# A tuned two-block network on one core: norm factors by tokens, the end on turned tokens, one weight unit split ahead of ada work

## The chip, the cores and the metric

The kernel runs on 1 core of one Trainium2 chip. The metric is the device time of one launch in microseconds (us). Each version is run three times or more, and the median counts. In the traces PE is the matmul engine (TensorE), DVE is VectorE, ACT is ScalarE, POOL is GpSimd and SP is SyncE. PEld is the loading of stationary operands into PE.

## What is computed

256 tokens of 1024 features go through two blocks, everything in float32. The first puts 16 meta tokens ahead, mixes by window means and a gated linear attention, and has a two-level mixture of experts. The second has two layers (l0, l1) over the 256 tokens `h` and 256 context tokens `hc`. The kernel spends most of its time there, and most of the change lies there.

```python
def _rms_norm(x, g):
    return x * lax.rsqrt(jnp.mean(x * x, axis=-1, keepdims=True) + EPS) * g
def _modulate(u, shift, scale):
    return u * (1.0 + scale) + shift
def _swiglu(u, w_gate, w_up, w_down):
    return (jax.nn.silu(u @ w_gate) * (u @ w_up)) @ w_down

h = rmsnorm(first_block(x, ...), final_norm_w)
for l in range(2):
    mod_x = silu(c) @ w_ada[l] + b_ada[l]     # nine vectors: shift, scale, gate of three sublayers
    h = h + 0.5 * g1 * _swiglu(_modulate(_rms_norm(h, norm_ffn1[l]), sh1, sc1), ffn1 weights)
    q, k, v = _modulate(_rms_norm(h, norm_mix[l]), shm, scm) @ w_in[l]
    h = h + gm * (attention(q, k, v, context) @ w_out[l])
    h = h + 0.5 * g2 * _swiglu(_modulate(_rms_norm(h, norm_ffn2[l]), sh2, sc2), ffn2 weights)
    # hc goes the same way with its own modulation; in the last layer only its keys and values count
return _rms_norm(h, norm_final)
```

## The kernel before

Activations lie turned. A tile has 128 features on the partitions and the tokens on the columns, 256 or 512 of them, and eight such rows make up the 1024 features. A product in float32 is made from two halves of each operand, high and low. `products` issues three matmuls for it: high by high (L1763), high weights by low rows (L1764) and low weights by high rows (L1765).

**Weights.** They stream through the kernel in units of up to 128x2048 elements (1 MB) in two slots. SP loads `raw`. ACT casts it to `w_hi` (`split_hi`, L589). DVE subtracts and gets `w_lo` (`split_lo`, L990). PE begins a unit when `lo_done` has reached it. A slot is loaded again when the high and the low part of the unit before it are done, and cast again when PE has finished with it. The order of each engine is written out by hand, stage by stage, and a counting semaphore joins each producer with its consumer.

**Ada work.** The modulation vectors `mod` are products of two single vectors (`c` and `c_ctx`) with the 75.5 MB of `w_ada`. ACT's queue loads a quarter chunk (`ada_load`, L607, when DVE is done with the one before it in that slot), DVE multiplies and adds (`ada_quarter`, L1008 and L1011), PE sums over partitions (`ada_sums`, L1930) and DVE adds the bias (L1020). These pieces are spread over the other stages. In `linear`, which does the query units and the out units, DVE takes the two accumulated tiles of a unit (L1559), does the ada quarters of that unit, and then makes `w_lo` for the unit two ahead.

**Norms.** The feature squares come from ACT (L615), and POOL sums six or seven of the eight rows in `sq_sum` (L1699). PE multiplies `ones_d` (a 128x128 matrix of 1/1024, in `base`) by the sum and by the last squares. That gives the mean on all partitions, 128x256 of it in a PSUM bank (`mean_of_sums` L1786, `mean_square` L1780, `half_mean_squares` L1821). ACT takes the root (L671, L638 or L653), and DVE the reciprocal, 128x256 in `rstd` (L1083, L1046 or L1026). Then DVE makes eight scaled rows `tmp_a` (`scaled_row`, L1069), ACT casts them and adds the shift (`high_rows`, L715, `u_hi`), and DVE makes their low part `u_lo` (`low_row`, L1076). The norms of the second block work in two halves, 256 tokens and 256 context tokens. The products that close the stage before (`close_down`, `close_linear`) and the first products of the next (`open_halves`) run around them. The norms have names: `ffn1` ahead of the router of the first block, `l0a`, `l0b`, `l0c` ahead of ffn1, attention and ffn2 of layer 0, `l1a`, `l1b`, `l1c` in layer 1, and `end2` at the end.

**The end.** After the last products of ffn2 of layer 1, DVE adds the last row to `h` (L1195) and ACT squares it. The norm `end2` follows on all of the eight rows. PE turns the result back to tokens on partitions (16 transposes, L1756), DVE copies it out of PSUM in four pieces (L1666), and SP stores it with one DMA (L568).

## Time and profile before

| | us |
|---|---|
| median of 3 runs | 2278.59 (2275.73 to 2281.95) |
| the profiled execution | 2279.42 |
| its span in the trace | 2277.7 |
| PE busy | 2192.4 |
| DVE busy | 1388.2 |
| ACT busy | 766.8 |
| POOL busy | 519.5 |

All times inside the program are from the profiled execution, in us from the start of its span. Its own time stands 1.7 above its span, and 0.8 above the median. The mean granted clock of PE over the span is 0.98 of full speed. A PE that waits shows as a gap between its rows, and the view of waits puts each gap down to the instruction that ended it.

### The profile page before, as it was taken

The page shows a single profiled execution, that of the slowest core. Times are in us where ns is not written, and L with a number is a line of the kernel's source. Part 1 is how long each engine was busy: PE and PEld are TensorE (multiplying, and loading weights), DVE is VectorE, ACT ScalarE, POOL GpSimd, SP SyncE. Part 2 cuts the span into 40 slices and gives each one's busy share as a digit, 9 for nine tenths or more (in the row PEclk, how much of TensorE's full clock was granted, in tenths as well). Part 3 has the DMA queues.
Part 4 walks back from the last instruction along what each step waited for, and adds up shares of the span by engine and source line. Part 5 has one row for each costly group of instructions (what it writes and reads, how often), then busy time and mean ns, then how long its engine had stood idle before and what let it go on. Part 6 is the DMA issues. An engine that isn't in the chain of part 4 may idle for free.

```text
span 2277.7 us, 31630 instructions
## 1 busy us (share of the span) xinstructions
PE 2192.4 (96%) x13181; PEld 1903.3 (84%) x13181; DVE 1388.2 (61%) x1780; ACT 766.8 (34%) x1073; POOL 519.5 (23%) x243
## 2 busy tenths in 40 slices
PE   7988999999999999999999999999999998999997
PEld 7868999988888888857888888888888887678997
DVE  5567877577776237695677773256654236765444
ACT  4334344432222222273422222142222223454443
POOL 0013633112221110153122221112222111143431
PEclk9889999999999999999999999999999999999999
DMA  5236886656664335401366652346663335205654
GB/s 160 93 94 166 219 220 193 182 160 182 172 174 135 89 103 174 111 20 39 101 191 174 177 167 82 105 112 185 185 185 113 96 90 168 74 12 153 181 165 121
DMA packets 473989, 314.67 MB, mean 138 GB/s; under 512 B 27488, under 2 KB 435943, under 8 KB 473847
## 3 DMA queue, kind: packets, MB, share of 16 engines
q1 hardware_dynamic: 434288, 237.02, 37.2%
q10 hardware_dynamic: 39558, 75.64, 10.7%
q8 instruction: 104, 1.70, 0.3%
q14 instruction: 39, 0.31, 0.0%
HBM read 311.56 MB, written 1.05 MB: 137 GB/s over the span
## 4 chain that ended last, share of the span: by engine, by line
PE 84%; DVE 9%; ACT 3%; DMA 1%; issue 1%; SPq 1%; POOL 0%; ACTq 0%; DVEq 0%; POOLq 0%
PE ps L1763 25%; PE ps L1765 25%; PE ps L1764 25%; DVE w_lo L990 3%; PE ps L1930 2%; ACT w_hi L589 2%; PE ps L1756 2%; PE ps L2340 1%; DVE st L1605 1%; DVE u_lo L1076 1%; PE ps L2302 1%; DVE tmp_a L1069 1%; DMA raw<-in_w_in 1%; SPq L562 1%; DMA raw<-in_w_ffn_down 1%
## 5 line engine op out<-in xcount | busy, mean ns | idle before, releaser
L1763 PE MATMUL ps<-u_hi,w_hi 128*128 128x256 f32 (+2 forms) x2624 | 890.0, 339 | 29.4 <-DVE w_lo L990 15.9
L1765 PE MATMUL ps<-u_hi,w_lo 128*128 128x256 f32 (+2 forms) x2624 | 878.1, 335 | 0.0
L1764 PE MATMUL ps<-u_lo,w_hi 128*128 128x256 f32 (+2 forms) x2624 | 878.0, 335 | 0.0
L990 DVE TENSOR_TENSOR w_lo<-raw,w_hi 128x2048 fp32r<-128x2048 f32 (+1 forms) x238 | 504.5, 2120 | 339.8 <-ACT w_hi L589 339.6
L589 ACT CAST w_hi<-raw 128x2048 fp32r<-128x2048 f32 (+1 forms) x238 | 418.0, 1757 | 468.9 <-PE ps L1765 420.5
L1763 PEld LDWEIGHTS ps<-u_hi,w_hi 128*128 128x128 f32 x2624 | 502.9, 192 | 84.1 <-DVE w_lo L990 21.8
L1765 PEld LDWEIGHTS ps<-u_hi,w_lo 128*128 128x128 f32 x2624 | 502.8, 192 | 48.8
L1764 PEld LDWEIGHTS ps<-u_lo,w_hi 128*128 128x128 f32 x2624 | 503.3, 192 | 46.9
L1684 POOL TENSOR_TENSOR hf_lo<-tmp_b,hf_hi 128x512 fp32r<-128x512 f32 (+1 forms) x88 | 240.4, 2732 | 715.5 <-ACT hf_hi L729 715.5
L1011 DVE SCALAR_TENSOR_TENSOR ada_acc<-ada_w,sc_c,ada_acc 128x512 f32<-128x512 f32 x448 | 347.4, 832 | 5.5
L726 ACT ACTIVATE tmp_a<-ps 128x512 f32<-128x512 f32 (+1 forms) x120 | 60.2, 501 | 704.9 <-PE ps L1765 540.5
L1763 PE MATMUL ps<-hf_hi,w_hi 128*128 128x512 f32 (+1 forms) x770 | 271.0, 352 | 1.3 <-DVE w_lo L990 1.1
L1764 PE MATMUL ps<-hf_lo,w_hi 128*128 128x512 f32 (+1 forms) x770 | 269.4, 350 | 0.0
L1765 PE MATMUL ps<-hf_hi,w_lo 128*128 128x512 f32 (+1 forms) x770 | 269.4, 350 | 0.0
L1137 DVE TENSOR_TENSOR tmp_b<-tmp_a,ps 128x512 f32<-128x512 f32 (+1 forms) x120 | 68.2, 568 | 183.6 <-ACT tmp_a L726 182.5
L1763 PEld LDWEIGHTS ps<-hf_hi,w_hi 128*128 128x128 f32 x770 | 144.9, 188 | 23.1 <-DVE w_lo L990 1.3
L1764 PEld LDWEIGHTS ps<-hf_lo,w_hi 128*128 128x128 f32 x770 | 144.9, 188 | 21.0
L1765 PEld LDWEIGHTS ps<-hf_hi,w_lo 128*128 128x128 f32 x770 | 144.9, 188 | 20.9
L1699 POOL TENSOR_TENSOR sq_sum<-sq_sum,tmp_b 128x512 f32<-128x512 f32 (+1 forms) x37 | 75.4, 2038 | 299.9 <-ACT tmp_b L615 252.5
L1744 POOL TENSOR_SCALAR s<-s,st 128x512 f32<-128x512 f32 (+1 forms) x48 | 78.9, 1646 | 141.8 <-DVE st L1620 141.8
L1684 POOL TENSOR_TENSOR hm_lo<-tmp_b,hm_hi 128x256 fp32r<-128x256 f32 x32 | 77.7, 2428 | 133.8 <-ACT hm_hi L729 133.8
L1195 DVE SCALAR_TENSOR_TENSOR h<-ps,gate,h 128x256 f32<-128x256 f32 x50 | 22.3, 480 | 104.3 <-PE ps L1765 104.3
(299 smaller groups left out, 1886.1 us busy)
## 6 DMA issues: line engine op xcount, KB each, us to landing
ada_w<-in_w_ada ACTq DMA_DIRECT2D x144, 512.0 KB, 3.9
raw<-in_w_ffn_gate SPq DMA_DIRECT2D x88, 512.0 KB, 4.0
raw<-in_w_ffn_up SPq DMA_DIRECT2D x88, 512.0 KB, 5.3
raw<-in_w_in SPq DMA_DIRECT2D x52, 512.0 KB, 4.9
raw<-in_w_ffn_down SPq DMA_DIRECT2D x64, 384.0 KB, 3.5
raw<-in_w_ffn_down SPq DMA_DIRECT2D x64, 320.0 KB, 4.2
raw<-in_w_expert_gate SPq DMA_DIRECT2D x32, 512.0 KB, 4.3
raw<-in_w_expert_up SPq DMA_DIRECT2D x32, 512.0 KB, 5.6
```

The source lines that it names most:

```text
L589: nc.scalar.copy(w_hi[:, slot, 0:elems], raw[:, slot, 0:elems]).then_inc(hi_done.sem, 1)
L726: nc.scalar.activation(tmp_a[:, n % 2, 0:T], ps[:, 2 * (g % 2), 0:T], ACT.Silu).then_inc(sig["silu"].sem, 1)
L990: tt(w_lo[:, slot, 0:elems], raw[:, slot, 0:elems], w_hi[:, slot, 0:elems].bitcast(F32), ALU.subtract).then_inc(lo_done.sem, 1)
L1011: ins = stt(out=ada_acc[:, v, :], in0=ada_w[:, slot, kk, :], scalar=sc_c[:, k, v:v + 1], in1=ada_acc[:, v, :], op0=ALU.mult, op1=ALU.add)
L1137: tt(tmp_b[:, n % 2, 0:T], tmp_a[:, n % 2, 0:T], ps[:, 2 * (g % 2) + 1, 0:T], ALU.mult).then_inc(acc_free.sem, 1)
L1684: tt(lo[:, n, 0:T], tmp_b[:, n % 2, 0:T], hi[:, n, 0:T].bitcast(F32), ALU.subtract).then_inc(sig["lo"].sem, 1)
L1699: tt(sq_sum[:, 0:T], sq_sum[:, 0:T], tmp_b[:, k % 2, 0:T], ALU.add).then_inc(n["summed"].sem, 1)
L1744: ins = nc.gpsimd.tensor_scalar(s[:, x, 1, c0:c1], s[:, x, 1, c0:c1], st[:, i % 4, 0, nq + q:nq + q + 1], None, ALU.mult)
L1756: return nc.tensor.transpose(dst, src, ident[0:n, 0:n])
L1763: mm(acc, w1, m_hi, start=(first and i == 0), stop=False)
L1764: mm(acc, w1, m_lo, start=False, stop=False)
L1765: ins = mm(acc, w2, m_hi, start=False, stop=(last and i == n - 1))
```

## The change

**Norms by tokens.** In `ffn1`, `l0b`, `l0c`, `l1a`, `l1b`, `l1c` and the latent half of `l0a` the mean is taken with the operands exchanged. The sums and squares are stationary, and one column of `ones_d` moves (`token_means`). The mean stands by tokens, 128 on the partitions and two columns for 256 tokens. ACT's root and DVE's reciprocal work on these two columns (`tok_inv`). PE then spreads the factor (`spread_factor`): a column of `tok_inv`, broadcast to 128x128, is stationary and the identity moves. The factor stands in a PSUM bank for 256 tokens on all partitions, where the scaled rows read it. The separate mean of the sums for both halves (`sums_of_halves`) goes, and the reciprocal of the second half moves from behind `w_lo` to ahead of it.

**The end.** ACT scales each row of `h` by the final weight as soon as it has been squared (`out_row`, into `h1`, which is free by then). PE turns it between the last products (`turn_out`). After the last row, mean, root and reciprocal are taken by tokens, on two columns. ACT and DVE each scale one half of the turned result by the token's factor on the way out of PSUM, and SP stores it with two DMAs.

**`linear`.** For the first unit of each of its stages, DVE makes `w_lo` ahead of the ada quarters.

```diff
+        BY_TOKENS = ("ffn1", "l0b", "l0c", "l1a", "l1b", "l1c")
...
-            sp.wait_ge(rows_out.sem, rows_out.at(12 + 4))
-            sp.dma_start(out[0].rearrange("(t p) d -> p t d", p=P), o_rows[:, :, :]).then_inc(st_out, 16)
-            sp.wait_ge(st_out, 16)
+            for t in range(2):
+                sp.wait_ge(ev["out_left"], t + 1)
+                sp.wait_ge(ev["out_right"], t + 1)
+                sp.dma_start(out[0, P * t:P * t + P, :], o_rows[:, t, :]).then_inc(st_out, 16)
+            sp.wait_ge(st_out, 32)
...
-                nc.scalar.activation(rstd[:, 0:T], ps[:, 5, 0:T], ACT.Sqrt, bias=eps).then_inc(n["root"].sem, 1)
+                if nm in BY_TOKENS:
+                    nc.scalar.activation(tok_inv[:, 0, :], ps[:, 5, 0:2], ACT.Sqrt, bias=eps).then_inc(n["root"].sem, 1)
+                else:
+                    nc.scalar.activation(rstd[:, 0:T], ps[:, 5, 0:T], ACT.Sqrt, bias=eps).then_inc(n["root"].sem, 1)
...
             def half_root(nm, q):
 
-                n, (c0, c1, v), F = norm_of[nm], HALVES[nm][q], WHOLE[nm]
-                act.wait_ge(n["ms"].sem, n["ms"].at((q + 1) * (KD - F)))
-                nc.scalar.activation(rstd[:, c0:c1], ps[:, 5 + q, c0:c1], ACT.Sqrt, bias=eps).then_inc(n["root"].sem, 1)
+                n = norm_of[nm]
+                act.wait_ge(n["ms"].sem, n["ms"].at(q + 1))
+                nc.scalar.activation(tok_inv[:, q, :], ps[:, 5 + q, 0:2], ACT.Sqrt, bias=eps).then_inc(n["root"].sem, 1)
 
...
+            def out_row(n):
+
+                k = n // 2 - 1
+                if n % 2 == 0 and k >= 0:
+                    w = VEC["final2"][0] + k
+                    nc.scalar.activation(h1[:, k, 0:SEQ], h2[:, k, 0:SEQ], ACT.Identity,
+                                         scale=vec[:, w:w + 1]).then_inc(norm_of["end2"]["w"].sem, 1)
...
+            n = norm_of["end2"]
+            act.wait_ge(acc_free.sem, acc_free.at(end_of(layers[1]["f2b"])))
+            square("end2", KD - 1, 1, h2, SEQ)
+            out_row(2 * KD)
+            act.wait_ge(n["ms"].sem, n["ms"].at(1))
+            nc.scalar.activation(row_inv[:, :], ps[:, 4:6, 0:1].rearrange("p t o -> p (t o)"), ACT.Sqrt,
+                                 bias=eps).then_inc(n["root"].sem, 1)
+            act.wait_ge(turned.sem, turned.at(11))
+            act.wait_ge(n["rstd"].sem, n["rstd"].at(1))
+            for t in range(2):
+                nc.scalar.activation(o_rows[:, t, 0:512], ps[:, OUT_BANKS[t][0], :], ACT.Identity,
+                                     scale=row_inv[:, t:t + 1]).then_inc(ev["out_left"], 1)
...
             def half_rstd(nm, q):
 
-                n, (c0, c1, v) = norm_of[nm], HALVES[nm][q]
+                n = norm_of[nm]
                 dve.wait_ge(n["root"].sem, n["root"].at(q + 1))
-                nc.vector.reciprocal(rstd[:, c0:c1], rstd[:, c0:c1]).then_inc(n["rstd"].sem, 1)
-                dve.wait_ge(n["rstd"].sem, n["rstd"].at(q + 1))
+                nc.vector.reciprocal(tok_inv[:, q, :], tok_inv[:, q, :]).then_inc(n["rstd"].sem, 1)
 
             def rows_from(nm, t0, q, k0, k1, ahead=2):
 
+                dve.wait_ge(norm_of[nm]["spread"].sem, norm_of[nm]["spread"].at(q + 1))
...
-                stt(out=scaled(q, k, c1 - c0), in0=(h2 if h is None else h)[:, k, first + c0:first + c1], scalar=s, in1=rstd[:, c0:c1],
+                stt(out=scaled(q, k, c1 - c0), in0=(h2 if h is None else h)[:, k, first + c0:first + c1], scalar=s,
+                    in1=rstd[:, c0:c1] if nm == "l0a" and q == 0 else ps[:, 5 + q, 0:SEQ],
...
                         add_half(1).then_inc(acc_free.sem, 1)
+                    if k == 5 and not whole:
+                        half_rstd(nm, 1)
                 if second and not whole:
                     split_lo(convert[-1], convert[-1] % 2, elems_of[convert[-1]])
-                if not whole:
-                    half_rstd(nm, 1)
                 if second and not whole:
                     rows_from(nm, t0, 1, 0, KD)
...
                     take(i, ps[:, 2 * (g % 2):2 * (g % 2) + 2, :]).then_inc(acc_free.sem, 1)
+                    convert = u + 2 < N_UNITS and not (keep_last and i == stg["units"] - 1)
+                    if convert and i == 0:
+                        split_lo(u + 2, u % 2, elems_of[u + 2])
                     for c, quarter in work:
                         ada_quarter(c, quarter)
-                    if u + 2 < N_UNITS and not (keep_last and i == stg["units"] - 1):
+                    if convert and i:
                         split_lo(u + 2, u % 2, elems_of[u + 2])
                     if behind:
...
-                nc.vector.tensor_copy(o_rows[:, t // 2, 512 * (t % 2):512 * (t % 2) + 512], ps[:, 2 + t, :]).then_inc(rows_out.sem, 1)
+            n = norm_of["end2"]
+            dve.wait_ge(n["root"].sem, n["root"].at(1))
+            nc.vector.reciprocal(row_inv[:, :], row_inv[:, :]).then_inc(n["rstd"].sem, 1)
+            dve.wait_ge(n["rstd"].sem, n["rstd"].at(1))
+            dve.wait_ge(turned.sem, turned.at(11))
+            for t in range(2):
+                ts(o_rows[:, t, 512:D], ps[:, OUT_BANKS[t][1], :], row_inv[:, t:t + 1], None,
+                   ALU.mult).then_inc(ev["out_right"], 1)
...
+            def token_means(nm, bank, c0, last):
+
+                for t in range(2):
+                    a = c0 + P * t
+                    mm(ps[:, bank, t:t + 1], sq_sum[:, a:a + P], ones_d[:, 0:1], start=True, stop=False)
+                    for (need_sq, slot, c) in last:
+                        if t == 0:
+                            need_sq()
+                        ins = mm(ps[:, bank, t:t + 1], tmp_b[:, slot, c + P * t:c + P * t + P], ones_d[:, 0:1], start=False,
+                                 stop=slot == 1)
+                return ins
+
+            def spread_factor(nm, q, bank, slot):
+
+                n = norm_of[nm]
+                pe.wait_ge(n["rstd"].sem, n["rstd"].at(q + 1))
+                for t in range(2):
+                    ins = mm(ps[:, bank, P * t:P * t + P], tok_inv[:, slot, t:t + 1].to_broadcast([P, P]), ident[:, :],
+                             start=True, stop=True)
+                ins.then_inc(n["spread"].sem, 1)
...
             def half_mean_squares(nm, q):
 
                 n, (c0, c1, v), F = norm_of[nm], HALVES[nm][q], WHOLE[nm]
-                for k in range(F, KD):
+
+                def squared(k):
                     pe.wait_ge(n["sq"].sem, n["sq"].at(k + 1 + q * (KD - F)))
-                    mm(ps[:, 5 + q, c0:c1], ones_d, tmp_b[:, k % 2, c0:c1], start=False, stop=(k == KD - 1)).then_inc(n["ms"].sem, 1)
+                pe.wait_ge(n["summed"].sem, n["summed"].at(F))
+                token_means(nm, 5 + q, c0, [(lambda k=k: squared(k), k % 2, c0) for k in range(F, KD)]).then_inc(n["ms"].sem, 1)
...
-                        ins = products(acc, uA % 2, [P * k for k in range(cut, kt2)], rows[cut:kt2], c1 - c0, False, False)
+                        products(acc, uA % 2, [P * k for k in range(cut, 7)], rows[cut:7], c1 - c0, False, False)
+                        spread_factor(nm, 0, 5, 0)
+                        ins = products(acc, uA % 2, [P * k for k in range(7, kt2)], rows[7:kt2], c1 - c0, False, False)
...
+            def turn_out(n):
+
+                k = n // 2 - 2
+                if n % 2 or k < 0:
+                    return None
+                w = norm_of["end2"]["w"]
+                pe.wait_ge(w.sem, w.at(k + 1))
+                for t in range(2):
+                    ins = turn(ps[:, OUT_BANKS[t][k // 4], P * (k % 4):P * (k % 4) + P], h1[:, k, P * t:P * t + P], P)
+                return ins
...
-            norm("end2", SEQ, KD - 1)
-
-            src = h2
-            w = norm_of["end2"]["w"]
-            pe.wait_ge(w.sem, w.at(8))
-            for t in range(4):
-                for k in range(4):
-                    kk = 4 * (t % 2) + k
-                    c = P * (t // 2)
-                    ins = turn(ps[:, 2 + t, P * k:P * k + P], src[:, kk, c:c + P], P)
-                ins.then_inc(turned.sem, 1)
+            n, tail = norm_of["end2"], (KD - 1) % 2
+            pe.wait_ge(n["summed"].sem, n["summed"].at(WHOLE["end2"]))
+            for t in range(2):
+                mm(ps[:, 4 + t, 0:1], sq_sum[:, P * t:P * t + P], ones_d[:, 0:1], start=True, stop=False)
+            pe.wait_ge(n["sq"].sem, n["sq"].at(KD))
+            for t in range(2):
+                ins = mm(ps[:, 4 + t, 0:1], tmp_b[:, tail, P * t:P * t + P], ones_d[:, 0:1], start=False, stop=True)
+            ins.then_inc(n["ms"].sem, 1)
+            turn_out(2 * KD)
+            turn_out(2 * KD + 2).then_inc(turned.sem, 1)
```

DVE at the first query units of layer 0 (`proj_107` is where the two accumulated tiles of a unit go), before and with the change:

```order
L1559 TENSOR_SCALAR proj_107<-ps 128x1024 [waits unit_done,dve_chain]
L1008 TENSOR_SCALAR ada_acc<-ada_w,sc_c 128x512 [waits ada_sum,ada_full_0]
L1008 TENSOR_SCALAR ada_acc<-ada_w,sc_c 128x512
L1011 SCALAR_TENSOR_TENSOR ada_acc<-ada_w,sc_c,ada_acc 128x512 [waits ada_mac] x2
L1011 SCALAR_TENSOR_TENSOR ada_acc<-ada_w,sc_c,ada_acc 128x512 [waits ada_mac,ada_full_1]
L1011 SCALAR_TENSOR_TENSOR ada_acc<-ada_w,sc_c,ada_acc 128x512 [waits ada_mac] x3
L990 TENSOR_TENSOR w_lo<-raw,w_hi 128x2048 [waits hi_done]
L1559 TENSOR_SCALAR proj_107<-ps 128x1024 [waits unit_done]
```

```order
L1598 TENSOR_SCALAR proj_107<-ps 128x1024 [waits unit_done,dve_chain]
L1018 TENSOR_TENSOR w_lo<-raw,w_hi 128x2048 [waits hi_done]
L1036 TENSOR_SCALAR ada_acc<-ada_w,sc_c 128x512 [waits ada_sum,ada_full_0]
L1036 TENSOR_SCALAR ada_acc<-ada_w,sc_c 128x512
L1039 SCALAR_TENSOR_TENSOR ada_acc<-ada_w,sc_c,ada_acc 128x512 [waits ada_mac] x2
L1039 SCALAR_TENSOR_TENSOR ada_acc<-ada_w,sc_c,ada_acc 128x512 [waits ada_mac,ada_full_1]
L1039 SCALAR_TENSOR_TENSOR ada_acc<-ada_w,sc_c,ada_acc 128x512 [waits ada_mac] x3
L1598 TENSOR_SCALAR proj_107<-ps 128x1024 [waits unit_done]
```

The `w_lo` of the third query unit has moved ahead of two L1008 and six L1011 (now L1036 and L1039), and it now stands right behind the first `proj_107`.

DVE around the second half of the norm `l0b`, before and with the change. In the new rows `ps` is the bank that holds the spread factor:

```order
L1069 SCALAR_TENSOR_TENSOR tmp_a<-h,coef,rstd 128x256 [waits norm_lo]
L1076 SCALAR_TENSOR_TENSOR u_lo<-tmp_a,mod,u_hi 128x256 [waits norm_hi] x2
L990 TENSOR_TENSOR w_lo<-raw,w_hi 128x2048 [waits hi_done]
L1083 RECIPROCAL rstd<-rstd 128x256 [waits norm_root]
L1069 SCALAR_TENSOR_TENSOR tmp_a<-h,coef,rstd 128x256 [waits norm_lo,norm_rstd]
L1069 SCALAR_TENSOR_TENSOR tmp_a<-h,coef,rstd 128x256 [waits norm_lo]
L1076 SCALAR_TENSOR_TENSOR u_lo<-tmp_a,mod,u_hi 128x256 [waits norm_hi]
```

```order
L1103 SCALAR_TENSOR_TENSOR tmp_a<-h,coef,ps 128x256 [waits norm_lo]
L1118 RECIPROCAL tok_inv<-tok_inv 128x2 [waits norm_root]
L1111 SCALAR_TENSOR_TENSOR u_lo<-tmp_a,mod,u_hi 128x256 [waits norm_hi] x2
L1018 TENSOR_TENSOR w_lo<-raw,w_hi 128x2048 [waits hi_done]
L1103 SCALAR_TENSOR_TENSOR tmp_a<-h,coef,ps 128x256 [waits norm_lo,factor_spread]
L1103 SCALAR_TENSOR_TENSOR tmp_a<-h,coef,ps 128x256 [waits norm_lo]
L1111 SCALAR_TENSOR_TENSOR u_lo<-tmp_a,mod,u_hi 128x256 [waits norm_hi]
```

The reciprocal has gone from 256 columns to two and from behind `w_lo` to ahead of the last two `u_lo`. The first scaled row of the second half now waits for PE (`factor_spread`).

PE at the very end, before and with the change:

```order
L1765 MATMUL ps<-hf_hi,w_lo 128x256
L1786 MATMUL ps<-sq_sum,base 128x256 [waits norm_summed]
L1780 MATMUL ps<-tmp_b,base 128x256 [waits norm_sq]
L1756 MATMUL ps<-base,h 128x128 [waits norm_w]
L1756 MATMUL ps<-base,h 128x128 x15
```

```order
L1807 MATMUL ps<-hf_hi,w_lo 128x256
L2471 MATMUL ps<-base,sq_sum 128x1 [waits norm_summed]
L2471 MATMUL ps<-base,sq_sum 128x1
L2474 MATMUL ps<-base,tmp_b 128x1 [waits norm_sq]
L2474 MATMUL ps<-base,tmp_b 128x1
L1798 MATMUL ps<-base,h 128x128 [waits norm_w]
L1798 MATMUL ps<-base,h 128x128
L1798 MATMUL ps<-base,h 128x128 [waits norm_w]
L1798 MATMUL ps<-base,h 128x128
```

The two matmuls of 256 columns are four of one column, and of the sixteen transposes four are left here. The other twelve now stand between the products of the last units, in pairs.

## Rows read from the trace of the kernel before

**Rows 1.** The page's first part: busy time of each engine, share, instructions

```profile
PE 2192.4 (96%) x13181; PEld 1903.3 (84%) x13181; DVE 1388.2 (61%) x1780; ACT 766.8 (34%) x1073; POOL 519.5 (23%) x243
```

**Rows 2.** Waits of PE: what for; us in total, times, longest

```profile
PE ps L1763 <- DVE w_lo L990: 20.2, 13, 5.9
PE ps L1763 <- DVE u_lo L1076: 9.3, 8, 4.1
```

**Rows 3.** Timeline, the end: start, us, engine, line, instruction [idle before <-releaser]

```profile
2260.38 0.48 DVE L1195 SCALAR_TENSOR_TENSOR h<-ps,gate,h 128x256 f32<-128x256 f32 x1 [4.54 <-PE ps L1765]
...
2261.36 0.70 PE L1780 MATMUL ps<-tmp_b,base 128*128 128x256 f32 x2 [0.59 <-ACT tmp_b L615]
2262.10 0.47 ACT L653 ACTIVATE rstd<-ps,base 128x256 f32<-128x256 f32 x1 [0.79 <-PE ps L1780]
2262.61 1.75 DVE L1026 RECIPROCAL rstd<-rstd 128x256 f32<-128x256 f32 x1 [1.75 <-ACT rstd L653]
...
2268.82 3.68 PE L1756 MATMUL ps<-base,h 128*128 128x128 f32 x16 [6.75 <-ACT h L660]
...
2272.53 0.69 DVE L1666 COPY o_rows<-ps 128x512 f32<-128x512 f32 x1 [0.16 <-PE ps L1756]
2273.25 0.39 SPq L568 DMA_DIRECT2D out<-o_rows  x1
```

**Rows 4.** The chain in order of time, two pieces: start, us, what

```profile
892.37 1.68 PE ps L1930 x16
...
1020.71 1.02 PE ps L1756 x8
```

**Rows 5.** Groups by form, DVE: count | busy, mean ns | idle before

```profile
L1020 DVE TENSOR_TENSOR mod<-ps,b_ada 128x8 f32<-128x8 f32 x28 | 4.4, 156 | 11.0 <-PE ps L1930 11.0
...
L1195 DVE SCALAR_TENSOR_TENSOR h<-ps,gate,h 128x256 f32<-128x256 f32 x50 | 22.3, 480 | 104.3 <-PE ps L1765 104.3
...
L1069 DVE SCALAR_TENSOR_TENSOR tmp_a<-h,coef_fin,rstd 128x256 f32<-128x256 f32 x8 | 3.7, 478 | 0.0
```

**Rows 6.** Timeline, ACT, a root on one column

```profile
2199.16 0.20 ACT L733 ACTIVATE root_one<-base 128x1 f32<-128x1 f32 x1
```

**Rows 7.** Timeline, ACT, early in the last stage (ffn2 down, layer 1)

```profile
2225.56 1.37 ACT L589 CAST w_hi<-raw 128x1408 fp32r<-128x1408 f32 x1 [4.00 <-DMA raw<-in_w_ffn_down]
```

**Rows 8.** Timeline, DVE, first query units of layer 0

```profile
871.36 1.22 DVE L1559 TENSOR_SCALAR proj<-ps 128x1024 f32<-128x1024 f32 x1 [3.20 <-PE ps L1765]
...
873.29 4.06 DVE L1011 SCALAR_TENSOR_TENSOR ada_acc<-ada_w,sc_c,ada_acc 128x512 f32<-128x512 f32 x6
877.27 2.29 DVE L990 TENSOR_TENSOR w_lo<-raw,w_hi 128x2048 fp32r<-128x2048 f32 x1
```

**Rows 9.** Timeline, ACT and its queue, the same stretch

```profile
871.34 1.90 ACT L589 CAST w_hi<-raw 128x2048 fp32r<-128x2048 f32 x1 [3.78 <-PE ps L1765]
874.73 3.03 ACTq L607 DMA_DIRECT2D ada_w<-in_w_ada  x2
```

**Rows 10.** Windows: A:B us, busy PE, PEld, DVE, ACT, POOL, PEclk, DMA share, GB/s

```profile
877.00:879.60 2.60, 0.01 (x1) 0.00 (x0) 2.60 (x3) 1.74 (x1) 0.00 (x0) 1.00 0.69 179
879.60:882.00 2.40, 2.39 (x7) 1.85 (x8) 2.40 (x4) 0.15 (x1) 0.00 (x0) 0.60 0.83 238
```

**Rows 11.** Tile ada_w, 860 to 930 us: landing time of its DMAs

```profile
DMA to landing us min/median/max: 3.6/3.8/5.2
```

**Rows 12.** Timeline, DVE, the norm l1c

```profile
2062.63 1.75 DVE L1083 RECIPROCAL rstd<-rstd 128x256 f32<-128x256 f32 x1 [2.17 <-ACT rstd L671]
```

**Rows 13.** Timeline, ACT, behind the root of the norm ffn1

```profile
150.91 1.89 ACT L589 CAST w_hi<-raw 128x2048 fp32r<-128x2048 f32 x1
```

**Rows 14.** Timeline, PE, means of the sums in the norm l0c

```profile
1101.65 1.13 PE L1786 MATMUL ps<-sq_sum,base 128*128 128x256 f32 x4 [0.73 <-POOL sq_sum L1699]
```

**Rows 15.** Timeline, DVE, second half of the norm l0b

```profile
857.13 2.28 DVE L990 TENSOR_TENSOR w_lo<-raw,w_hi 128x2048 fp32r<-128x2048 f32 x1
```

**Rows 16.** Timeline, ACT, the norm l1b

```profile
1883.51 3.69 ACT L589 CAST w_hi<-raw 128x2048 fp32r<-128x2048 f32 x2
```

79 lines of the change are left out of this document (42 added, 37 removed).

## The prediction

> **What bounds the kernel now.** Read in this order: the busy shares, the list of who waited for whom on PE, then the timeline at each norm. PE is busy 96% of the span [rows 1]. A change that takes work off DVE or ACT therefore pays only where PE stands still. PE's own waits are short and of two kinds: for the low part of a weight unit (w_lo, DVE), 20.2 us in 13 waits, and for the low part of a normalized row (u_lo, DVE), 9.3 us in 8 [rows 2]. Beside these stands the end, where PE has no products left: from the last accumulate, 2260.38, to the end of the span, 2277.7, are 17.3 us in which one engine after the other works [rows 3]. The reciprocal over 128x256 is the longest piece, 1.75 us; the eight scaled rows follow, then 3.68 us of turning, the last copy, and the store, whose issue stands 4.45 us before the end.
>
> **The prices** [rows 4 to 6]. A float32 matmul with one moving column costs two records: 16 records of the ada sums take 1.68 us, 0.105 each, so 0.21 per matmul. A 128-column transpose takes 0.13 (8 in 1.02). A float32 matmul of 128 columns has two such records; I take 0.26, so a spread of two costs 0.52. A small DVE instruction takes 0.16 us (128x8), a small ACT one 0.20. So root and reciprocal on two columns take 0.36 instead of 0.47 + 1.75, and the spread adds 0.52 and a semaphore's way of about 0.1: the chain from mean to first row gets 1.2 us shorter. The reciprocal on two columns itself is in no row; its bounds are the 0.16 and the 1.75, and I take 0.16, since duration goes with columns in every other DVE row.
>
> **The end.** Before, as above, 17.3 us. After: the accumulate and the square stay (to 2261.3, where the mean began at 2261.36 [rows 3]), two one-column matmuls 0.45, root 0.25, reciprocal 0.2: the factor is there at 2262.25. The rows are already scaled by the weights and turned, the last pair while root and reciprocal run; the last row's ACT scaling (0.5) ends at 2261.8 and delays neither. Two DVE passes of 128x512 at 0.69 end at 2263.7, ACT's two beside them earlier. From the issue of the store to the end took 4.45 us for 1 MB; now half of it leaves 0.7 us earlier. Bounds 3.6 and 4.45, taken 4.0: end at 2267.7, **10.0 us saved**. Against it stand twelve transposes between the products of the last stage. Early in that stage the weights come late (ACT waits 4.0 us for a DMA [rows 7], and PE waits for w_lo just behind it), which covers the first four; eight at 0.13 are new work on a full PE: **+1.0**. The added ACT row (0.5 us, seven times before the last products) goes into waits of 2 to 4 us as in [rows 7] and costs nothing; without that cover it would push w_hi, and so PE, by up to 3.5. Net −9.0, bounds −7 and −10.5.
>
> **The third query unit of layer 0.** DVE takes the products of the first unit at 871.36, then does 4.9 us of ada work to 877.35, and only then w_lo for the third [rows 8], though ACT had w_hi ready at 873.25 [rows 9]. PE stands from 877.0 to 879.6 and then runs at a granted clock of 0.60 from 879.6 to 882 [rows 10], the lower of the two levels for part of it: the wait of 2.6 us costs a further 1.7 (the unit took 12.7 us where the next took 11.0). With w_lo first it is done at 875.6 and both go: −4.3. What is late next: ada work now ends near 880.4, so the second pair of ada loads, which ACT issued at 874.73 and again at 877.4 [rows 9], is issued some 3 us later, the second at 880.4. A load lands in 3.6 to 5.2 us [rows 11], here beside 1 MB of weights, so at 884 to 885.6; ACT's cast for the fourth unit stands behind that issue, and DVE's w_lo for it behind the ada work: 2.7 us more, then 2.3, so 889 to 890.7. PE comes free of the third unit at 888.1, does the ada sums until 889.9 and waits at most 0.8. Fourth unit 3.3 to 4.0 us earlier: I take −3.7; bounds −1 (if the clock falls again) and −4.3. The out stage of layer 0 is turned round in the same way; PE waits for nothing there, so it counts zero.
>
> **The norms inside the kernel.** Each saves only what its last-ending wait lets go:
> - Before ffn2 of layer 1 (l1c) PE has nothing else: its wait for u_lo is 4.1 of the 9.3 us, and the 1.75 of the reciprocal stands in it [rows 2, 12]. The chain shortens by 1.2; everything behind is tied to the DVE rows: −1.2.
> - Before the router (ffn1) the same chain, but ACT's cast of a weight unit follows the root, 150.91 to 152.8 [rows 13]. It now begins 0.25 earlier, and the first u_hi waits for it: −0.8 instead of −1.2. In l0a the same pattern gives −0.4.
> - Ahead of ffn2 in layer 0 (l0c) PE waited 0.73 for the sums and spent 1.13 on them, in front of half a unit's products [rows 14]. Sums move behind those products. Gone: 1.5 (with overlap) and 1.03 of means; come: six matmuls of 0.21 and one spread of 0.52: −0.8, and the rest of that closing is tied to it.
> - l0b and l1a: −0.2 each by the same count with four one-column matmuls. The second half's reciprocal leaves DVE, but it stood behind the w_lo PE waits for, which begins at 857.13 because of the rows ahead of it [rows 15]. The new small reciprocal falls into a gap there, the new spread into PE's wait of 1.2. So nine of the large reciprocals go and most were hidden anyway.
> - l1b: here the reciprocal stands ahead of w_lo, and 1.75 would go. But ACT's two casts start at 1883.51, the first ends 1885.4 [rows 16], and w_lo started at 1885.8: −0.4. ACT is late next.
> Together −3.2 − 0.8 = **−4.0**: 1.2 + 0.8 + 0.4 + 0.8 + 0.4 + 0.4.
>
> **A rule against it.** The scaled rows now read the factor from PSUM. In the rows a 128x256 scalar_tensor_tensor takes 480 ns with PSUM as source and 478 without [rows 5]: I charge nothing. The Trainium skill, page "VectorE: DVE Perf Modes", section "The TRN2 errata", gives VectorE a fixed term of 120 cycles for a PSUM source against 58 for SBUF, which at 0.96 GHz would be an estimated 65 ns more for each row, 3.6 us in seven places of eight rows. The rows of this trace disagree with it.
>
> **Sum.** −9.0 − 3.7 − 4.0 = −16.7. The profiled execution took 2279.42 (span 2277.7), 0.8 above the median of 2278.59; against the median, **2261.9 us**, −0.73%. About 0.3%, 6.8 us, is what a measurement of this kernel can tell from no change.
>
> **Rivals.**
> - A (12%): the query stage gives its gain back. For it: ada loads and 1 MB of weights share the DMA engines. Against: the landings of 3.6 to 5.2 us were measured beside such a load. One wait of 2.7 at the fourth unit, with a clock loss of 1.0 kept: 2265.6.
> - B (9%): PSUM as a source slows the rows. Rows of this very shape differ by up to 50 ns between groups; eight rows in seven chains that DVE bounds: +2.8, 2264.7. The page named above would put it at 2265.5.
> - C (8%): ACT's extra rows and the transposes hold up the last stage, whose weights already come late: seven times 0.5 in front of w_hi: +3.5, 2265.4.
> - D (7%): the clock. Every shift moves the stretches at the lower level; each one that falls onto products costs about 1.7 as in the query stage. Two more: 2265.3; two fewer: 2258.5.
> - E (4%), slower: PE now holds the round trip. Each of the ten spreads inside the program waits in PE's queue for ACT and DVE, with all products behind it. If the small reciprocal comes behind a w_lo of 2.29 us [rows 8], PE loses that each time: +22.9 − 16.7 = +6.2, 2284.8. It decides from an average loss of 1.7 us per spread. Against it: four to six products' time stands between mean and spread, 1.4 us or more, and the chain needs 0.5.
> - F (2%): the small reciprocal and root take as long as the large (a fixed cost). Then the end gives 8, the query stage 3.7, and the norms lose the spreads: 2268.
>
> **Numbers.** The forecast has 58%. A to D lie within 4 us of it. The range 2256.5 to 2269.0 takes in the bounds of the end (+2/−1.5), of the query stage (+2.7/−0.6), one or two shifts of the clock (1.7 each) and the median's own scatter (the three runs span 6 us); outside are E, F and the tails, 2 in 10. Faster by over 0.3%: forecast, A to D and F less a tail, 0.93; within 0.3%: 0.03; slower: 0.04.
>
> **What would show it.** After the last product about 7.5 us instead of 17.4; two stores; transposes in pairs between products. No PE wait for w_lo at the third query unit, a granted clock of 1.0 behind it, and the fourth unit starting within 1 us of the ada sums' end. Reciprocals of 0.16 us, spreads of 0.5. PE's wait for u_lo in l1c split in two, 2.8 in all; the waits of 1.0 and 1.2 in l0b and l1a still there; l1b's 3.0 down to about 2. It is wrong if PE stalls ahead of the spreads by more than 0.3 us each, if the rows take over 0.5 us, or if the last stage takes more than 1.5 us longer.

## The result, and the profile after

The changed kernel takes 2264.75 us (median of 5 runs, 2263.07 to 2266.74), the kernel before 2280.28 in the same measurement. The ratio is 0.9935, 95% interval 0.9922 to 0.9948. Run a second time unaltered, it took 2266.47 us, ratio 0.9947 (0.9935 to 0.9959). The forecast was 2261.9 us, 0.9927 of the median that stood on record before (2278.59), with a range up to 2269.0.

The page's first part and the waits of PE, after, answer to [rows 1, 2]:

```profile
PE 2189.6 (97%) x13281; PEld 1906.8 (84%) x13281; DVE 1369.8 (61%) x1770; ACT 764.9 (34%) x1075; POOL 519.6 (23%) x243
```

```profile
PE ps L1805 <- DVE w_lo L1018: 15.0, 12, 5.9
...
PE ps L1805 <- DVE u_lo L1111: 6.9, 5, 2.3
```

DVE's busy time fell by 18.4 us, PE's by 2.8, and the span by 14.8. DVE was not what bounded the kernel, so most of what it lost was no gain; the table below shows where it was one. Of PE's waits, 5.2 us went from those for `w_lo` and 2.4 from those for `u_lo`.

The timeline of the end, after, answers to [rows 3]:

```profile
2255.51 0.48 DVE L1231 SCALAR_TENSOR_TENSOR h<-ps,gate,h 128x256 f32<-128x256 f32 x1 [4.95 <-PE ps L1807]
...
2256.49 0.61 PE L2474 MATMUL ps<-base,tmp_b 128*128 128x1 f32 x4 [0.69 <-ACT tmp_b L623]
...
2256.96 0.64 PE L1798 MATMUL ps<-base,h 128*128 128x128 f32 x4
2257.14 0.26 ACT L994 ACTIVATE row_inv<-ps,base 128x2 f32<-128x2 f32 x1 [0.30 <-PE ps L2474]
2257.43 0.17 DVE L1703 RECIPROCAL row_inv<-row_inv 128x2 f32<-128x2 f32 x1 [1.44 <-ACT row_inv L994]
2257.69 1.26 ACT L999 ACTIVATE o_rows<-ps,row_inv 128x512 f32<-128x512 f32 x2 [0.29 <-PE ps L1798]
2257.70 1.41 DVE L1707 TENSOR_SCALAR o_rows<-ps,row_inv 128x512 f32<-128x512 f32 x2
2258.53 1.01 SPq L576 DMA_DIRECT2D out<-o_rows  x2
```

From the last accumulate to the end of the span (2262.9) are 7.4 us, before 17.3. The reciprocal takes 0.17 us on two columns. What is left is one pass out of PSUM and the stores, of which the first is issued 4.4 us before the end.

**Where the time went, stage by stage.** Every trace holds the same 11046 products in the same order. So I take the start of a product in one trace less its start in the first trace of before. The table shows how much that distance changes from one product to the next mark; negative is faster. `b.again` is the kernel before, run a second time, and `again` the changed kernel, run a second time. The other columns are experiments, told below. A stage counts up to the first products behind its norm.

```
to               b.again   norms  q_only     end   after   again   q_old
start to router     2.50    0.04   -0.72    3.05   -2.52    1.26   -0.90
experts             0.02    0.03   -0.01   -0.01    0.75    0.01    0.01
l0a                 0.01   -0.44    0.00    0.00   -0.44   -0.44   -0.44
l0b                -0.02    0.02    0.00   -0.01    0.01    0.02    0.01
query l0            0.03    0.05   -2.26    0.05   -1.97   -1.87   -1.59
attention l0       -0.01    0.16   -0.01    0.01   -0.01    0.02   -0.00
l0c                 0.01   -0.63    0.00    0.00   -0.85   -0.63   -0.85
l1a                 0.01    0.03    0.00    0.00    0.03    0.03    0.03
l1b                 1.38    0.72    0.45    1.39   -0.37   -0.37   -0.36
query, key l1      -0.51   -1.72    1.44   -0.85   -0.68   -0.98   -0.81
attention l1       -0.03    1.75   -0.02   -0.02    1.05    1.15    1.13
l1c                -0.14    0.31    0.21   -0.01   -0.55    0.32   -0.38
ffn2 l1            -0.80   -0.62   -0.01    0.51    0.68    0.45    0.72
end of span         0.02    0.01   -0.00   -9.52   -9.89   -9.89   -9.89
sum                 2.48   -0.29   -0.94   -5.40  -14.76  -10.92  -13.31
```

Three things are to be seen. Most of layer 0 repeats to 0.02 us from trace to trace, so terms of half a microsecond can be read there that no total would show. The first stage, layer 1 from `l1b` on, and the last feed-forward differ by 0.2 to 3.8 us between two traces of one kernel. A single pair of traces does not tell what the change did in those.

The third is attention in layer 1. It is 1.05 to 1.82 us longer in eight of the ten traces of versions with the norms by tokens, and within 0.03 us in all four others. In every trace the granted clock falls in that stage: 39 to 40 us behind the stage's start in the six traces that agree, and 45 to 48 us behind it in the eight. The prediction's sum has no such term. Whether the change draws the fall there is not shown.

The stage of the third query unit, DVE, after; it answers to [rows 8]:

```profile
871.07 2.29 DVE L1018 TENSOR_TENSOR w_lo<-raw,w_hi 128x2048 fp32r<-128x2048 f32 x1 [0.69 <-ACT w_hi L597]
...
874.07 4.06 DVE L1039 SCALAR_TENSOR_TENSOR ada_acc<-ada_w,sc_c,ada_acc 128x512 f32<-128x512 f32 x6
878.05 1.22 DVE L1598 TENSOR_SCALAR proj<-ps 128x1024 f32<-128x1024 f32 x1
880.48 5.39 DVE L1039 SCALAR_TENSOR_TENSOR ada_acc<-ada_w,sc_c,ada_acc 128x512 f32<-128x512 f32 x8 [1.21 <-DMA ada_w<-in_w_ada]
885.79 2.28 DVE L1018 TENSOR_TENSOR w_lo<-raw,w_hi 128x2048 fp32r<-128x2048 f32 x1
```

The windows around the fourth unit, after (as [rows 10]: busy PE, PEld, DVE, ACT, POOL, clock, DMA share, GB/s):

```profile
884.00:886.00 2.00, 1.79 (x9) 1.18 (x7) 2.00 (x4) 0.00 (x0) 0.00 (x0) 1.00 0.82 207
886.00:888.00 2.00, 1.87 (x16) 1.78 (x16) 2.00 (x2) 1.63 (x1) 0.00 (x0) 1.00 0.56 128
888.00:890.00 2.00, 1.87 (x5) 1.55 (x6) 2.00 (x6) 0.27 (x1) 0.00 (x0) 0.63 0.74 222
890.00:892.00 2.00, 2.00 (x6) 1.51 (x6) 2.00 (x5) 0.00 (x0) 0.00 (x0) 0.52 1.02 344
```

The third unit no longer waits. The ada load is late, as said: ACT issued it at 875.52, and DVE waited 1.21 us for it, to 880.48. The `w_lo` for the fourth unit is there at 888.07. Ahead of it PE has the one-column ada sums and some tenths of waiting, and behind it the granted clock is 0.63 and 0.52. So the wait of 2.6 us is gone, and the fall of the clock that stood behind it now stands behind the sums. The fourth unit's first product starts 3.6 us earlier against the stage's start than before, which is the forecast 3.7, and then the fall takes 1.6 us of it back.

The groups by form, after, for the spread factor and its readers (count | busy, mean ns | idle before):

```profile
L1103 DVE SCALAR_TENSOR_TENSOR tmp_a<-h,coef,ps 128x256 f32<-128x256 f32 x72 | 33.4, 475 | 6.6 <-PE ps L1847 6.6
...
L1838 PE MATMUL ps<-base,tmp_b 128*128 128x1 f32 x60 | 10.2, 254 | 2.5 <-ACT tmp_b L693 1.7 <-ACT tmp_b L623 0.3
...
L1103 DVE SCALAR_TENSOR_TENSOR tmp_a<-h,coef,rstd 128x256 f32<-128x256 f32 x8 | 4.9, 606 | 0.0
L1103 DVE SCALAR_TENSOR_TENSOR tmp_a<-h,coef_fin,ps 128x256 f32<-128x256 f32 x8 | 3.7, 474 | 1.5 <-PE ps L1847 1.5
```

Rows that read the factor from PSUM take 474 and 475 ns, against 478 from SBUF in [rows 5]. The eight rows with a mean of 606 ns are those of the context half of `l0a`, which still read SBUF. The mean is that of one slow row and seven of the usual time (474 to 477 ns), the slow one being this:

```profile
395.21 1.53 DVE L1103 SCALAR_TENSOR_TENSOR tmp_a<-h,coef,rstd 128x256 f32<-128x256 f32 x1
```

The kernel before has the same slow row at the same place, so it has nothing to do with the change.

### The profile page after: what moved, and what is told of

Its sections match the earlier page's. It is cut to its first block, busy times and chain, and to the rows that moved or that the text cites. A ratio compares the mean times of both kernels' runs of the same rounds, so it can differ in the third digit from the quotient of the medians.

```text
span 2262.9 us, 31830 instructions
## 1 busy us (share of the span) xinstructions
PE 2189.6 (97%) x13281; PEld 1906.8 (84%) x13281; DVE 1369.8 (61%) x1770; ACT 764.9 (34%) x1075; POOL 519.6 (23%) x243
## 3 DMA queue, kind: packets, MB, share of 16 engines
q10 hardware_dynamic: 39558, 75.64, 10.9%
HBM read 311.56 MB, written 1.05 MB: 138 GB/s over the span
## 4 chain that ended last, share of the span: by engine, by line
PE 86%; DVE 8%; ACT 3%; DMA 1%; issue 1%; SPq 0%; POOL 0%; DVEq 0%; ACTq 0%
PE ps L1805 26%; PE ps L1807 25%; PE ps L1806 25%; DVE w_lo L1018 2%; PE ps L1987 2%; ACT w_hi L597 2%; PE ps L1798 2%; PE ps L2417 1%; PE ps L2379 1%; DVE st L1644 1%; DVE u_lo L1111 1%; DMA raw<-in_w_in 1%; DVE tmp_a L1103 1%; PE ps L2385 1%; DVE ada_acc L1039 1%
## 5 line engine op out<-in xcount | busy, mean ns | idle before, releaser
L1039 DVE SCALAR_TENSOR_TENSOR ada_acc<-ada_w,sc_c,ada_acc 128x512 f32<-128x512 f32 x448 | 347.4, 831 | 6.7 <-DMA ada_w<-in_w_ada 1.2
```

Of the source, the lines that this page charges most:

```text
L1039: ins = stt(out=ada_acc[:, v, :], in0=ada_w[:, slot, kk, :], scalar=sc_c[:, k, v:v + 1], in1=ada_acc[:, v, :], op0=ALU.mult, op1=ALU.add)
```

## Experiments

The table above, for the versions that stand in none of its columns; rows that tell nothing of them are left out, so the sums hold more than the rows:

```
to                  late   q_mid   turns  store1   comb.  comb.2
l0b                 0.55    0.03    0.02    0.02    0.02    0.03
query l0           -2.08   -4.44   -2.26   -2.03   -4.41   -4.41
attention l0        0.05    1.50   -0.03   -0.01    0.90    2.63
l0c                -0.32   -0.63   -0.64   -0.63   -0.56   -0.86
l1a                 0.60    0.03    0.03    0.03    0.03    0.02
l1b                -0.15    0.89    1.02   -0.37    0.22   -0.36
query, key l1      -0.52   -0.20   -2.29   -0.27   -3.25   -2.33
ffn2 l1             0.12    0.71    0.80    0.33    0.50   -0.11
end of span        -9.89   -9.89   -8.57   -9.19   -9.89   -9.89
sum               -15.47  -11.60   -9.30   -9.44  -15.63  -14.57
```

**The changed kernel once more**, for the scatter between traces.

> The changed kernel a second time, unaltered. It shows how far two profiled executions of one program differ stage by stage. Theory 1 (the differences between the traces of before and after are the change's own, apart from the program's start): the products between the first norm of the second block and the last one start at the same distances from each other within 0.3 us a stage, the fourth query unit of layer 0 again has the clock at its lower level for about 4 us, and in the query units of layer 1 the wait of 2.3 us and the clock's fall behind it are there again. Theory 2 (part of it is scatter): the clock's falls in layer 1 and the 1.3 us lost in the experts are at other places or gone. Time by both: within 3 us of 2264.75.

Measured: 2266.47 us, 0.9947 (0.9935 to 0.9959); column `again` above. Most of the second block's stages repeat, the fall at the fourth query unit and the one in the query units of layer 1 too. But the 0.75 us in the experts is gone, and the first stage is 3.8 us longer. Falls of the clock at 128 and 1110 us are new. Both theories hold, each for its own part of the table.

One stage that does not repeat is the change's own: `l1c`, -0.55 in one trace and 0.32 in the other. The spread there, in the first trace and in the second:

```profile
2057.86 0.71 PE L1847 MATMUL ps<-base,tok_inv 128*128 128x128 f32 x4 [0.62 <-DVE tok_inv L1118]
```

```profile
2061.42 1.22 PE L1847 MATMUL ps<-base,tok_inv 128*128 128x128 f32 x4 [0.62 <-DVE tok_inv L1118]
```

The granted clock during it is 1.00 in the first and 0.50 in the second. From the end of the squares to the first scaled row are 2.47 us in the first and 3.35 in the second, against 3.28 in both traces of before. The new chain has matmuls where the old one had a reciprocal, so it gains 0.8 us at the upper level of the clock and nothing at the lower, or loses up to 0.4. Of the ten traces with norms by tokens, four have the upper level there (2.47 to 2.48 us), six the lower for part or all of it (3.18 to 3.69).

**The kernel before once more.**

> The kernel before, unaltered, for a second trace. Theory 1 (where the clock falls inside the second block belongs to a program): granted clock of 0.5 to 0.6 for about 3.4 us behind the wait of 2.6 us at the third query unit of layer 0, and again at 1934 to 1938 in layer 1, as in its first trace. Theory 2 (the place of a fall varies from one execution to the next): the third query unit at full clock behind the same wait, as in the version with the old order of linear, or a fall at another place such as 1110 or 1890; each costs or returns 1.4 to 1.9 us. Stages without a fall agree within 0.1 us by both.

Measured: one run, 2281.87 us; column `b.again`. The windows of the kernel before in its second trace, and below them in its first:

```profile
882.00:884.00 2.00, 1.87 (x6) 1.52 (x7) 2.00 (x4) 0.28 (x1) 0.00 (x0) 0.78 0.74 217
884.00:886.00 2.00, 2.00 (x6) 1.56 (x5) 2.00 (x4) 0.00 (x0) 0.00 (x0) 0.50 1.00 348
1890.00:1892.00 2.00, 1.28 (x6) 1.28 (x7) 1.97 (x4) 0.00 (x0) 0.00 (x0) 0.51 0.08 15
...
1934.00:1936.00 2.00, 2.00 (x10) 1.68 (x9) 0.00 (x0) 0.00 (x0) 1.82 (x1) 1.00 1.10 372
```

```profile
1890.00:1892.00 2.00, 2.00 (x19) 2.00 (x19) 1.91 (x3) 0.45 (x2) 0.00 (x0) 1.00 1.02 355
...
1934.00:1936.00 2.00, 1.72 (x5) 1.48 (x6) 2.00 (x1) 1.07 (x3) 1.87 (x1) 0.70 0.01 3
```

The fall behind the third query unit is there in both. The one in layer 1 is at 1934 in the first trace and at 1890 in the second, with the same program. So a place of a fall in layer 1 is no property of the kernel. The one at 1934 costs 1.8 us, the one at 1890, which is longer, 2.7, of which the table has 1.38 in `l1b` and the rest in the next stage. Theory 2 holds for layer 1; for the query units of layer 0 theory 1 does, in these two.

**The new order in `linear`, taken out of the changed kernel, and put alone into the kernel before.**

```diff
-                    if convert and i == 0:
-                        split_lo(u + 2, u % 2, elems_of[u + 2])
                     for c, quarter in work:
                         ada_quarter(c, quarter)
-                    if convert and i:
+                    if convert:
                         split_lo(u + 2, u % 2, elems_of[u + 2])
```

> The change without its part in linear: w_lo of the third query unit again behind the ada work. Theory 1 (the trace of after: 4.4 us won at the third unit, 2.2 given back at the fourth, where PE stands shortly before it and the clock falls): the wait of 2.6 us and the clock's fall stand at the third unit, the fourth runs at full clock, and the stage is 2.1 us longer than in the changed kernel, so 2.1 us slower, ratio to before 0.9944. Rival (the prediction: 3.7 us, as the fall at the fourth unit is not owed to the new order): 3.7 us slower, ratio 0.995, and a fall of the clock at the fourth unit here too.

> The kernel before with nothing but the new order in linear. Theory 1: 2.1 us faster than before, with the clock's fall at the fourth unit instead of the third; ratio 0.9991. Rival (3.7 us, the clock falls in neither unit): ratio 0.9984. In the trace the two differ by the granted clock in the 4 us behind the ada sums: 0.55 or so by theory 1, 1.0 by the rival.

Measured: without it 2267.4 us, 0.9954 (0.9942 to 0.9966); with it alone 2277.16 us, 0.9997 (0.9986 to 1.0007). Alone it makes the stage 2.26 us shorter (column `q_only`), with the fall at the fourth unit: theory 1, and not the 3.7 us of the prediction. Its total can't be told from no change. Without it (`q_old`) neither theory's picture came. The wait of 2.6 us is back, but no fall stands behind it. These are the windows of that version, the wait and what follows:

```profile
875.70:878.30 2.60, 0.00 (x0) 0.00 (x1) 2.60 (x3) 1.75 (x1) 0.00 (x0) 1.00 0.67 193
878.30:880.70 2.40, 2.40 (x11) 1.99 (x11) 2.40 (x4) 0.14 (x1) 0.00 (x0) 1.00 0.68 218
```

Set beside [rows 10], with the same wait and the same work on DVE: 0.60 there, 1.00 here. So the same wait of 2.6 us is sometimes followed by a fall and sometimes not, and the stage then differs by 1.6 us. Against this trace the new order is worth 0.4 us, against the traces with a fall 1.9 to 2.3. What decides it stays open.

**The new end alone**, in the kernel before (the parts on `end2`, `out_row`, `turn_out` and the two stores).

> The kernel before with nothing but the new end (rows weighted and turned between the last products, root and reciprocal on two columns, scaling on the way out, two stores). Theory 1 (the traces: 9.7 to 9.9 us off the end, 0.7 put into the last stage by transposes): 9.0 us faster, ratio 0.9961, and 7.4 us from the last accumulate to the end of the span. Rival (the transposes cost nothing and the 0.7 was the last stage's weights coming at other times): 9.8 us faster, ratio 0.9957, and the last products end as late after the first of their stage as in the kernel before, within 0.3 us.

Measured: 2270.53 us, 0.9968 (0.9956 to 0.9981), that is 4.3 to 10 us faster. The end itself is 9.52 us shorter. The last stage is 0.51 longer than in the first trace of before and 1.3 longer than in the second, so the stage sums can't settle what the transposes cost. Its steps can. In the traces of the changed kernel the distance to before grows by 0.21 to 0.23 us at each pair, five times in this stage, 1.09 in all, and nowhere so in the next experiment. The rival falls. (In the changed kernel the end is shorter by another 0.37 us. Here DVE begins its pass out of PSUM 0.4 us behind ACT, there with it; why is not shown.)

**All sixteen transposes behind the last products.**

```diff
-            turn_out(2 * KD)
+            for m in range(4, 2 * KD + 2, 2):
+                turn_out(m)
             turn_out(2 * KD + 2).then_inc(turned.sem, 1)
```

> The changed kernel with all sixteen transposes behind the last products. Theory 1 (the twelve between the products cost PE 0.7 us in the last stage, and behind it they would stand on the path): the last stage 0.7 us shorter, then sixteen transposes at 0.16 take 2.6 us instead of 0.64, of which the root and the reciprocal no longer cover more than before: 1.9 us later, net 1.2 us slower than the changed kernel. Rival (they cost nothing between the products): net 1.9 us slower. From the last accumulate to the end 9.3 us instead of 7.4.

Measured: 2266.38 us, 0.994 (0.9926 to 0.9954), no different from the changed kernel. The turning at the end, in that version:

```profile
2261.10 1.94 PE L1798 MATMUL ps<-base,h 128*128 128x128 f32 x16
```

The sixteen take 1.94 us, 0.12 each and not 0.16. The end is 1.32 us longer than in the changed kernel (-8.57 against -9.89) where 1.9 was expected, and the steps of 0.22 are gone. To turn between the products costs 1.1 and saves 1.3. That part of the change is worth 0.2 us.

**One store in place of two.**

> The changed kernel with one store of 1 MB in place of two of half that. Theory 1 (before: 4.45 us from issue to the end of the span for one; after: 3.9 us from the issue of the second of two): the only store is issued at the time of the second, plus 0.1, and ends 0.6 us later. Rival (a store's time is in its completion, not in its bytes): no difference, within 0.1 us. Both are read from the trace; the total can't tell them apart.

Measured: 2268.4 us, 0.9947 (0.9934 to 0.9961).

```profile
2263.80 0.39 SPq L575 DMA_DIRECT2D out<-o_rows  x1
```

In the changed kernel the second of the two stores is issued here:

```profile
2259.19 0.36 SPq L576 DMA_DIRECT2D out<-o_rows  x1
```

Both issues stand 4.0 us behind the start of the last product. From the single store's to the end of the span (2268.2) are 4.4 us, from the second of two (2262.9) 3.7. The end is 0.70 longer (-9.19 against -9.89), all of it behind the issue. Theory 1 holds, with 0.7 in place of 0.6: issued at the same time, the store of half the bytes is done sooner.

**The norms by tokens alone**, with the old end and the old order.

> The kernel before with nothing but the norms by tokens and their spread; old end, old order in linear. Theory 1 (stage by stage in the traces of the changed kernel): 0.7 us at the router, 0.44 in l0a, 0 in l0b and l1a, 0.75 in l0c, 0.37 in l1b, 0.5 in l1c, together 2.8 us, and the third query unit waits 2.6 us as before; ratio 0.9988. By the prediction: 4.0 us, ratio 0.9982. The version with the old order in linear ran its third query unit at full clock behind that wait: if this comes from the norms, 1.7 us more go here (0.9980); if it is scatter, it may or may not be there.

Measured: 2280.0 us against 2281.49, 0.9992 (0.9981 to 1.0003). Column `norms`: 0.44 in `l0a`, 0 in `l0b` and `l1a`, 0.63 in `l0c` with a fall behind it. The third query unit has its wait and its fall (0.05), so that the missing fall in `q_old` does not come from the norms. In layer 1 falls hide most of the rest, and in `l1c` the spread met the lower clock (1.22 us, the chain 3.50). The norms by themselves are a gain too small for the total to show.

**The small reciprocal behind `w_lo`**, rival E put to the test.

```diff
-                    if k == 5 and not whole:
-                        half_rstd(nm, 1)
                 if second and not whole:
                     split_lo(convert[-1], convert[-1] % 2, elems_of[convert[-1]])
+                if not whole:
+                    half_rstd(nm, 1)
```

> The changed kernel with the second half's two-column reciprocal put back behind w_lo, where the large one stood (l0b, l0c, l1a, l1b). PE holds the round trip now. Theory 1 (trace of after: w_lo ends 857.2, the spread was at 856.0 and the next products waited until 857.3 anyway): the spread comes at 857.4, the products behind it at 858.0, 0.75 us later, the scaled rows 0.85 later, in each of four norms: about 3 us slower, ratio 0.9956. Rival E's price of the prediction (the whole of w_lo, 2.29 us each): 9 us slower, ratio 0.998.

Measured: 2266.02 us, 0.9935 (0.9921 to 0.9948), no different from the changed kernel. DVE and PE in `l0b` of that version:

```profile
854.01 2.29 DVE L1018 TENSOR_TENSOR w_lo<-raw,w_hi 128x2048 fp32r<-128x2048 f32 x1
856.21 0.16 DVE L1118 RECIPROCAL tok_inv<-tok_inv 128x2 f32<-128x2 f32 x1
...
856.42 0.71 PE L1847 MATMUL ps<-base,tok_inv 128*128 128x128 f32 x4 [1.26 <-DVE tok_inv L1118]
857.17 0.87 DVE L1103 SCALAR_TENSOR_TENSOR tmp_a<-h,coef,ps 128x256 f32<-128x256 f32 x2 [0.80 <-PE ps L1847]
```

PE now waits 1.26 us for the reciprocal. But the wait of 0.67 that stood behind the spread is gone, since `w_lo` and rows are in time, and against the changed kernel `l0b` is 0.54 longer, `l1a` 0.57 and `l0c` 0.53. In `l1b` nothing is lost: up to the first products behind the norm the two traces agree within 0.02 us, and the 0.22 between the columns is the start of a fall that this trace has there. Together 1.7 us, below both prices that were set. The mechanism of the rival is real, its price of a whole `w_lo` for each spread is not: what stalls PE early spares it the stall behind.

**`w_lo` first for every query unit, the ada sums inside the fourth.**

```diff
+                    early = i == 0 or ada == "q"
-                    if convert and i == 0:
+                    if convert and early:
...
+                        inner = ada_of_unit(ada, i - 1)[1] if ada == "q" and i == 3 else None
-                        two_tiles(..., ready if i == 0 else None, c0)
+                        two_tiles(..., ready if i == 0 else None, c0, inside=inner)
```

> The changed kernel with w_lo ahead of the ada work for every query unit of layer 0, and the first ada sums put between the products of the fourth unit instead of ahead of it. Theory 1 (the fourth unit stands for w_lo, 888.07, and the clock falls where PE has only one-column sums before it): w_lo of the fourth unit is there at 883, it starts when the third ends, without wait or fall, and the stage is 2.2 us shorter than in the changed kernel; ratio 0.993. Rival (a later sum holds up DVE, whose next ada work waits for it, and PE waits for the fifth unit's w_lo or for the last sums instead): no gain, with a wait of 1 us or more at the first key unit.

Measured: 2265.94 us, 0.9934 (0.9921 to 0.9948). The query stage is 4.44 us shorter than before, 2.5 more than in the changed kernel, with a clock of 1.0 throughout: theory 1. But a fall at 980 us in the attention behind it gives 1.5 back, and falls in layer 1 the rest, so the total did not move.

**Combined with two roots ahead of a cast.** In the key and value units ACT takes the roots of the query norms ahead of `split_hi` and not behind it.

```diff
                     u = stg["u0"] + i + 2
+                    if ahead:
+                        ahead(i)
                     if u < N_UNITS and not (keep_last and i == stg["units"] - 1):
                         split_hi(u, u % 2, elems_of[u])
```

> The version with w_lo first and the ada sums inside the fourth unit, and beside that ACT takes the two roots of the query norms behind the first key and value units ahead of a cast of w_hi, for which PE waited 1.1 to 2.3 us in layer 1 and 0.48 in layer 0. Theory 1 (the cast is the last thing in that wait): the waits ahead of the rotation of the queries go below 0.3 us, the cast comes 0.8 us later and has 8 us of slack, 1.3 us faster than the version it builds on; ratio 0.9925. Rival (the third unit's load of weights, late behind the bias loads on SP's queue, is what ACT waits for there): no gain in layer 1 beyond what is gone anyway, and PE waits at the third key unit instead.

> The combined version a second time, unaltered. Theory 1 (its gain over the changed kernel is the wait at the fourth query unit and the one ahead of the rotation, 2.4 and 1.1 us): ratio 0.9925 within 0.0013 again. Rival (the first result was a fast draw): ratio 0.994, that of the changed kernel. In the trace the stages without a fall of the clock agree within 0.1 us with its first trace by both.

Measured: 2263.77 us, 0.9926 (0.9913 to 0.9939), and again 2261.99 us, 0.9916 (0.9902 to 0.9929). ACT there, in this version, and in the one it builds on:

```profile
1927.61 0.91 ACT L926 ACTIVATE tmp_b<-ps,base 128x256 f32<-128x256 f32 x2 [10.05 <-PE ps L2349]
1928.42 1.90 ACT L597 CAST w_hi<-raw 128x2048 fp32r<-128x2048 f32 x1
```

```profile
1929.18 1.90 ACT L597 CAST w_hi<-raw 128x2048 fp32r<-128x2048 f32 x1 [10.39 <-DMA raw<-in_w_in]
1930.99 0.83 ACT L929 ACTIVATE tmp_b<-ps,base 128x256 f32<-128x256 f32 x2
```

The wait of 1.1 to 2.3 us in layer 1 is gone. The roots no longer stand behind a cast that itself waits for a load. In layer 0 the wait of 0.48 went, but 0.5 to 0.7 us came ahead of the last ada sums and 0.59 at a later unit, 0.9 us more in all (column `comb.`). So the new order may be better kept to layer 1; that was not tried. Both of its results lie below the lower of the changed kernel's two; as intervals overlap, that it is faster than the changed kernel by some 0.2% is likely and not certain. It is clearly faster than the kernel before.

## Why the prediction was right, and where it was not

The time came within the range, 2.85 us (0.13%) above the forecast, and the largest term, the end, came by the forecast's own mechanism. Two terms fell short: the query unit by 1.7 us and the norms by 0.8 or more. Term by term, the norms' sizes from stages that repeat and from chains:

- **The end, -10.0 and +1.0**: measured -9.89 and +1.09. The chain ran as written, mean, root, reciprocal, one pass, stores. Transposes took 0.11 to 0.12 us each and not 0.13. The cover for the first four was less than assumed: ten and not eight counted.
- **The third query unit, -3.7**: measured -2.0 (bounds were -1 and -4.3). Against the one trace that had the wait without a fall it is -0.4. The step that was mis-sized is that the clock's fall would go with the wait. The wait went; a fall moved to the fourth unit, which the text had named as the lower bound ("if the clock falls again") and not taken. Its neighbour steps, that the ada loads come late and the fourth unit still starts 3.3 to 4.0 us earlier, were right (3.6).
- **The norms, -4.0**: the table and the chains give 0.7 at the router, 0.44 in `l0a`, 0 in `l0b` and `l1a` (0.2 each was forecast), 0.85 in `l0c`, 0.37 in `l1b`, 0.8 in `l1c` (1.2 forecast), together 3.2. That is with the upper level of the clock in `l1c`; with the lower level `l1c` gives nothing and the sum is at most 2.4. The prediction priced the spread at one clock only. What else was mis-sized in `l1c` can be read from its chain. (The prediction speaks of nine large reciprocals that go and ten spreads inside the program; it is eleven of each.)

PE, ACT and DVE in `l1c`, after, against [rows 12]:

```profile
2055.41 0.72 ACT L693 ACTIVATE tmp_b<-h 128x256 f32<-128x256 f32 x2 [4.08 <-DVE h L1693]
...
2056.65 0.58 PE L1838 MATMUL ps<-base,tmp_b 128*128 128x1 f32 x4
2057.27 0.26 ACT L682 ACTIVATE tok_inv<-ps,base 128x2 f32<-128x2 f32 x1 [1.14 <-PE ps L1838]
2057.64 0.17 DVE L1118 RECIPROCAL tok_inv<-tok_inv 128x2 f32<-128x2 f32 x1 [2.19 <-ACT tok_inv L682]
...
2058.60 0.87 DVE L1103 SCALAR_TENSOR_TENSOR tmp_a<-h,coef,ps 128x256 f32<-128x256 f32 x2 [0.80 <-PE ps L1847]
```

The spread between the last two is the line of 2057.86 shown above. The end of the squares and the first row in the kernel before:

```profile
2060.41 0.72 ACT L682 ACTIVATE tmp_b<-h 128x256 f32<-128x256 f32 x2 [4.08 <-DVE h L1654]
...
2064.41 0.88 DVE L1069 SCALAR_TENSOR_TENSOR tmp_a<-h,coef,rstd 128x256 f32<-128x256 f32 x2
```

From the end of the squares to the first row are 2.47 us, before 3.28. The spread takes 0.71 us where 0.52 was priced, the root 0.26 for 0.20. And the second token tile takes its sums and squares one after the other once the squares are there: the means end 1.1 us behind the squares, before 0.9, a term that the sum did not have.

- **PSUM as a source** (rival B): 475 ns against 478. The rule of the Trainium skill on the fixed term of a PSUM source (page "VectorE: DVE Perf Modes", section "The TRN2 errata") does not show in this form of instruction here either; the measurement decides. Rival B falls, though its 2264.7 us is the nearest number of all: that is luck. The 50 ns between groups that it went by separate other rows of 128x256, the `u_lo` rows (528 ns), from these.
- **Rival A** (a wait of 2.7 us at the fourth unit): no such wait, but 1.6 of its price of 3.7 us came, as clock. In its mechanism it was the nearest of the rivals.
- **Rival C** (the last stage held up by ACT's rows and the transposes, +3.5): beyond the transposes the stage is no longer than before. A wait for `w_lo` of about 1 us stands in it, in the first trace of before at 2228.65 (1.07 us), in its second nowhere, and in the changed kernel earlier, at 2211.16 (0.96) and 2214.97 (0.71).
- **Rival D** (the clock): it can't be told from the forecast by the total. In the traces it is the largest scatter there is, mostly 1.4 to 2.7 us for a fall that meets products.
- **Rival E**: PE stalls ahead of two of the eleven spreads, 0.55 us at the router and 0.62 in `l1c`. That is above the 0.3 us that the prediction set as a sign of being wrong; its other two signs, rows over 0.5 us and a last stage 1.5 us longer, did not come. With the small reciprocals behind `w_lo` the cost was 1.7 us, not 9.
- **Rival F**: the small reciprocal takes 0.17 us.

The measured terms sum to -9.9 + 1.1 - 2.0 - 3.2 = -14.0 us. The two traces of after lie 14.8 and 10.9 under the first of before and 17.2 and 13.4 under the second, 14.1 in the mean. That these agree so well is luck in part: the traces also hold attention in layer 1 (+1.1), the moved falls around `l1b` and a first stage that differs by 3.8 us, which are in no term. The totals of the three parts run alone (ratios 0.9968, 0.9997, 0.9992) multiply to 0.9957, a smaller gain than the 0.9935 to 0.9947 of the whole; with 0.0013 of uncertainty in each this is no contradiction, and shows that parts of 1 to 3 us can't be added up from totals of this kernel.

## What to carry to other kernels

When a kernel's order is fixed, line up two traces by a repeated instruction and read the change stage by stage. Run both kernels a second time first: only what repeats is the change's. A large operation that leaves a busy engine is worth only what its last-ending wait lets go (here eleven reciprocals of 1.75 us went for 2.4 to 3.2 us, and the end, where nothing else ran, gave 9.9). Count a fall of the clock behind a wait as a thing apart from the wait: it may go, stay or move to the next thin place. And where work moves from DVE to PE in a stretch in which PE has long been waiting, price it at the lower clock too: the spread in `l1c` took 0.71 or 1.22 us.

## What the runs showed of the hardware that was not expected

- The same wait of PE of 2.6 us, with the same work around it, was followed by a fall of the granted clock to the lower of its two levels in two traces of the kernel before, in the norms' version and in that of the end (0.60 over the next 2.4 us in the first), and by 1.00 in one of a version with the same code there. Between two traces of one kernel a fall to 0.5 changed its place from 1934 to 1890 us.
- Four matmul records of 128 columns took 0.60 us in nine of the eleven spreads, and at the two where PE had been waiting for most of the time before, 0.71 us at a granted clock of 1.00 and up to 1.22 at the lower level.
- A wait moved ahead can shorten one behind it: PE stood 1.26 us longer ahead of the spread, and the stage grew by 0.55.
- Scaled rows of 128x256 that read the factor from PSUM took 474 to 475 ns in their groups, those that read it from SBUF 478. A group's mean can hide one row: 606 ns was seven of 474 to 477 and one of 1.53 us. What slows that one was not tried.
